# The head of a hybrid encoder kernel: x loaded by quarters of its columns and turned between the products of the first projection

## The chip, the core and the metric

The kernel runs on one core of one Trainium2 chip. The metric is the device time of one execution in microseconds (us); the time before is the median of three runs. The profile is one further execution, taken by the hardware profiler. The engines are named PE (TensorE), PEld (its weight loads), DVE (VectorE), ACT (ScalarE), POOL (GpSimd) and SP (SyncE, which here only issues transfers).

## The reference, cut to what matters

```
def _rmsnorm(x, g):
    y = xf * lax.rsqrt(jnp.mean(xf * xf, axis=-1, keepdims=True) + EPS)
    return (y * g).astype(x.dtype)

def reference(x, ...):                       # x: 1 x 512 tokens x 1024
    for layer in range(2):
        h = _rmsnorm(x, mix_norm[layer])
        if layer % 2 == 0:
            x = x + _even_mixer(h, even_w_in[j], ...)   # proj = h @ w_in (1024 x 5376), attention, out projection
        else:
            x = x + _odd_mixer(h, ...)                  # gated recurrence
        x = x + _swiglu(_rmsnorm(x, ffn_norm[layer]), ...)
    return _rmsnorm(x, final_norm)
```

In `_even_mixer` the first 768 columns of `proj` are the queries (512), key (128) and value (128) of a grouped attention whose queries and keys are RMS-normalised per head. The other 4608 columns belong to a second group of heads.

## The kernel before

All products are made in three passes: an operand is split into a rounded half (`h_hi`, `w_hi`) and the remainder (`h_lo`, `w_lo`), and `mm3` adds hi·hi, hi·lo and lo·hi into one bank of PSUM (`ps`, eight banks of 512 columns). Each engine runs its own hand-written list of instructions in order; semaphores join them.

The weights come in chunks through a ring of four: SP loads chunk c into `stage` when POOL has finished chunk c-4 (`chunk_lo`), ACT rounds it into `w_hi` (`conv`, needs the products of chunk c-4 to be over, `chunk_used`), and POOL takes the remainder `w_lo` (`lo`). Chunks 0 to 15 are the first projection: for each step k of 0 to 7, one chunk of 512 and one of 256 columns, six tiles of 128 columns and so 18 products of 128x512. Chunks 16 to 111 are four head pairs of 24 chunks each (384 columns, 9 products a chunk).

x comes as four tokens-by-1024 blocks (`x_tok`, one load per block c). PE turns each block by eight 128x128 transposes (`x_turn`), and DVE and ACT copy the turned blocks from PSUM into `x_t` (channels on partitions). The first projection works on x times the norm's gain without the norm's per-token factor: `raw_high` (ACT) and `raw_low` (DVE) make the halves of that. The factor is brought in later where the queries, keys and values are used. For the head pairs the properly normalised h is needed:

- ACT squares the four blocks of x with a running sum (`x_sq`), DVE and ACT make 1/sqrt of the mean (`rstd`), DVE spreads it on a diagonal (`spread`), and PE broadcasts it over the partitions with a product into bank 7 (L2097, after step k = 3; `first_rb`).
- DVE copies it out (`rstd_a`) and makes, for each k, `h_scaled(k)` (into a ring of three `h_f`). ACT rounds it (`high(k)`, when step k's products no longer need the raw half), and DVE takes the remainder (`h_lo_part(k)`).
- Chunk 16+k of the first pair waits for `h_lo_part(k)`.

Small parameters come by twelve loads (`params_in`) and are turned on PE after step 5 (L2100); DVE copies them (L1272, `params_ready`), and the first pair's products wait for that. Then the outputs of the first projection leave PSUM in `first_pair`: ACT copies the value (`v_f`) and the key and squares the key. DVE scales the four query tiles (`aq_f`, L1345), and ACT squares each (`sq_qk`). PE sums the squares by head with tiny products (L2111): the key's ahead of the pair's step j = 2, the first query tile's ahead of j = 3. `x_spill` stores `x_t` to memory (2 MB) behind chunk 19.

Of the kernel before, what the change touches and what calls it, by code (L numbers as in the profile page):

```python
# [226 lines left out]

SWAP_A = [(i + 16) % 32 for i in range(32)]
# [64 lines left out]
def build(nc, A, out):  # L293
# [4 lines left out]
    with ctx:  # L298
# [36 lines left out]
        x_sq = at("x_sq", Z + 16 * K, [D])  # L335
# [69 lines left out]
        consts_in, mix_in, params_in, x_in = sem("consts_in"), sem("mix_in"), sem("params_in"), [sem(f"x_in{c}") for c in range(NC)]  # L405
# [3 lines left out]
        mix_gain_in, x_by_dve, x_by_act = sem("mix_gain_in"), sem("x_by_dve"), sem("x_by_act")  # L409
# [34 lines left out]
        x_rows = A["x"][0].rearrange("(i c) d -> c i d", c=NC)  # L444
# [63 lines left out]
        def _(sync):  # L508
# [10 lines left out]
            for c in range(NC):  # L519
                sync.dma_start(x_tok[:, c, :], x_rows[c]).then_inc(x_in[c], 16)  # L520
            for c in range(C_PAIR):
                k = c // 2
                col, n = (512, 256) if c % 2 else (0, 512)
                load(c, c, stage[:, c % RING, 0:n], w_even[rows(k), col:col + n])
                if c == 4:
                    sync.dma_start(head_sel[:, :], A["consts"][:, K_HEAD:K_HEAD + 2]).then_inc(params_in, 16)
                    for at_, name, n in ((G_FFN, "ffn_norm", 16), (G_FINAL, "final_norm", 8),
                                         (CONV_W, "odd_conv_w", 32), (CONV_B, "odd_conv_b", 8), (GA_B, "odd_gate_a_b", 16),
                                         (GX_B, "odd_gate_x_b", 16), (LAM, "odd_lambda", 16)):
                        v = A[name]  # L530
# [5 lines left out]
                if c == 7:  # L536
                    sync.dma_start(tab(K_COSA, 2 * T), A["consts"][:, K_COSA:K_COSB]).then_inc(table_a_in, 16)
                if c == 9:
                    sync.dma_start(tab(K_COSB, 2 * T), A["consts"][:, K_COSB:K_MASK]).then_inc(table_b_in, 16)
                if c == 11:  # L540
                    sync.dma_start(tab(K_MASK, NC * T), A["consts"][:, K_MASK:K_ALL]).then_inc(masks_in, 16)

            for p in range(4):
                for j in range(PAIR_CHUNKS):
                    t, k = divmod(j, KD)
                    c = C_PAIR + p * PAIR_CHUNKS + j
                    dst = stage[:, c % RING, 0:384].rearrange("p (g d) -> p g d", g=3)
# [173 lines left out]
        def _(act):  # L721
# [96 lines left out]
            def raw_high(k):  # L818

                if k == 0:  # L820
                    act.wait_ge(mix_gain_in, 1)
                    act.wait_ge(x_by_dve, 3)
                act.wait_ge(x_by_act, 1 + k // 4)
                act.activation(h_hi[:, k, :], x_t[:, k, :], ACT.Copy, scale=params[:, G_MIX + k:G_MIX + k + 1]).then_inc(h_hi_done, 1)
# [8 lines left out]
            act.wait_ge(x_turned, 2)  # L833
            act.activation(x_t[:, :, P:2 * P], ps[:, 2:4, :].rearrange("p b (j t) -> p (b j) t", t=P), ACT.Copy).then_inc(x_by_act, 1)
            convs(0, 1)
            act.wait_ge(x_turned, 4)
            act.activation(x_t[:, 4:8, 3 * P:4 * P], ps[:, 7, :].rearrange("p (j t) -> p j t", t=P), ACT.Copy).then_inc(x_by_act, 1)
# [3 lines left out]
            convs(2, 4)  # L841
            for k in range(2, KD):
                raw_high(k)
            for c in range(NC):
                act.wait_ge(x_in[c], 16)
                if c:
                    act.wait_ge(first_ss, c)
                act.activation(x_sq[:, :], x_tok[:, c, :], ACT.Square, accum_out=rstd[:, c:c + 1]).then_inc(first_ss, 1)
                if c == 1:
                    convs(4, 6)  # L850
            act.wait_ge(first_ms, 1)
            act.activation(rstd[:, :], rstd[:, :], ACT.Sqrt).then_inc(first_sqrt, 1)
            for k in range(KD):
                if k:
                    convs(2 * k + 4, 2 * k + 6)
                for i in {2: (0,), 3: (1, 2), 4: (3, 4)}.get(k, (k,) if k > 4 else ()):
                    high(i)
# [354 lines left out]
        def _(dve):  # L1212
# [14 lines left out]
            def x_in_place(c):  # L1227

                dve.wait_ge(x_turned, c + 1)
                b0 = 4 if c == 2 else 6  # L1230
                V.tensor_copy(x_t[:, :, c * P:(c + 1) * P], ps[:, b0:b0 + 2, :].rearrange("p b (j t) -> p (b j) t", t=P)).then_inc(x_by_dve, 1)

            def raw_low(k):

                dve.wait_ge(h_hi_done, k + 1)
                V.scalar_tensor_tensor(out=h_lo[:, k, :], in0=x_t[:, k, :], scalar=params[:, G_MIX + k:G_MIX + k + 1],  # L1236
                                       in1=h_hi[:, k, :].bitcast(f32), op0=ALU.mult, op1=ALU.subtract).then_inc(h_lo_done, 1)
# [11 lines left out]
            x_in_place(0)  # L1249
            dve.wait_ge(mix_turned, 1)  # L1250
            V.tensor_copy(params[:, 0:G_FFN], ps[:, 1, 0:G_FFN]).then_inc(mix_gain_in, 1)
            x_in_place(2)
            dve.wait_ge(x_turned, 4)
            V.tensor_copy(x_t[:, 0:4, 3 * P:4 * P], ps[:, 6, :].rearrange("p (j t) -> p j t", t=P)).then_inc(x_by_dve, 1)
            for k in range(KD):
                raw_low(k)
            dve.wait_ge(first_ss, NC)
            V.tensor_scalar(rstd[:, :], rstd[:, :], 1.0 / D, EPS, ALU.mult, ALU.add).then_inc(first_ms, 1)
            dve.wait_ge(first_sqrt, 1)
# [10 lines left out]
            h_lo_part(KD - 2)  # L1270
            dve.wait_ge(params_turned, 1)
            step.mark(V.tensor_copy(params[:, G_FFN:P], ps[:, 6, G_FFN:P]))  # L1272
            V.tensor_copy(qk_gain[:, :], ps[:, 6, P:P + 2]).then_inc(params_ready, 1)
            h_lo_part(KD - 1)
# [770 lines left out]
        def _(pe):  # L2045
# [18 lines left out]
            def x_turn(c):  # L2064

                pe.wait_ge(x_in[c], 16)
                if c == 3:
                    pe.wait_ge(x_by_dve, 1)
                b0 = (6, 2, 4, 6)[c]
                for j in range(KD):  # L2070
                    last = pe.transpose(ps[:, b0 + j // 4, (j % 4) * P:(j % 4 + 1) * P], x_tok[:, c, j * P:(j + 1) * P], ident[:, :])
                last.then_inc(x_turned, 1)
# [4 lines left out]
            x_turn(0)  # L2077
            pe.wait_ge(mix_in, 16)
            pe.transpose(ps[:, 1, 0:G_FFN], mix_rows[0:G_FFN, :], ident[0:G_FFN, 0:G_FFN]).then_inc(mix_turned, 1)
            x_turn(1)  # L2080
            x_turn(2)
            x_turn(3)
            idle_products(6)

            for k in range(KD):
# [8 lines left out]
                if k == 3:  # L2094
                    pe.wait_ge(ones_set, 2)
                    pe.wait_ge(first_diag, 1)
                    pe.matmul(ps[:, 7, :], ones[:, :], diag[:, 0, :, :].rearrange("p c q -> p (c q)"), start=True, stop=True).then_inc(first_rb, 1)  # L2097
                if k == 5:
                    pe.wait_ge(params_in, 16 * 12)
                    pe.transpose(ps[:, 6, 0:P], p_rows[:, :], ident[:, :])  # L2100
# [447 lines left out]
```

## Time and profile before

| | |
|---|---|
| three runs | 1270.55, 1270.8, 1273.13 us; median 1270.8 |
| the profiled execution | 1271.04 us; its span 1269.2 us |
| mean granted TensorE clock | 0.996 of full speed |
| busy: PE, PEld, DVE | 1252.1 us (99%), 1003.1 (79%), 840.4 (66%) |
| busy: ACT, POOL | 663.8 us (52%), 401.9 (32%) |

Times in the rows are microseconds from the span's start, unless marked ns. A matmul's row ends later than the next one starts, since they are pipelined: the pace is the distance of the starts. What stands in brackets at the end of a row is the idle time of the engine before it, and what ended it.

### The profile page before, as it was taken

How to read it: one execution, taken by the hardware profiler on the slowest of the kernel's cores; microseconds unless marked ns; L12 is line 12 of the kernel's file. 1: busy time of each engine (PE TensorE's matmuls, PEld its weight loads, DVE VectorE, ACT ScalarE, POOL GpSimd, SP SyncE). 2: the span in 40 equal slices, each digit the busy share in tenths (PEclk: the TensorE clock that was granted, in tenths of full speed). 3: DMA queues.
4: the chain of work that ended last, by engine and by line, in shares of the span. 5: the costliest groups of instructions: out<-in, count | busy, mean ns of one | idle time of the engine just before them, and what ended most of it. 6: DMA issues, size and time to landing. Idle time of an engine off the chain costs nothing.

```text
span 1269.2 us, 17728 instructions
## 1 busy us (share of the span) xinstructions
PE 1252.1 (99%) x6473; PEld 1003.1 (79%) x6473; DVE 840.4 (66%) x1328; ACT 663.8 (52%) x1214; POOL 401.9 (32%) x327
## 2 busy tenths in 40 slices
PE   8999999999999999999999999999979999999998
PEld 6877787777778888888888887777868888888886
DVE  4965765666636889898531156999888899972211
ACT  5454444444436665655532357786556655563233
POOL 4575563645625000000344443430300000024442
PEclk9999999999999999999999999999989999999999
DMA  6522222221244432330322345224443422122232
GB/s 208 169 72 66 64 63 64 59 68 56 57 137 149 142 133 100 133 100 1 93 83 92 100 136 163 67 67 150 150 149 100 133 88 78 67 75 83 84 100 92
DMA packets 101039, 126.60 MB, mean 100 GB/s; under 512 B 5976, under 2 KB 63576, under 8 KB 100312
## 3 DMA queue, kind: packets, MB, share of 16 engines
q1 hardware_dynamic: 100920, 125.45, 30.9%
q8 instruction: 52, 0.85, 0.3%
q14 instruction: 35, 0.29, 0.1%
q10 hardware_dynamic: 32, 0.01, 0.0%
HBM read 119.15 MB, written 6.29 MB: 99 GB/s over the span
## 4 chain that ended last, share of the span: by engine, by line
PE 89%; DVE 5%; issue 2%; ACT 2%; DMA 1%; SPq 1%; POOL 0%; POOLq 0%; DVEq 0%; ACTq 0%
PE ps L2048 26%; PE ps L2050 26%; PE ps L2049 26%; PE ps L2487 2%; PE ps L2402 2%; PE ps L2146 1%; PE ps L2158 1%; PE ps L2169 1%; PE ps L2204 1%; DMA w_stage<-in_even_w_in_dram 1%; DMA w_stage<-in_even_w_out_dram 1%; PE ps L2181 1%; PE ps L2185 1%; DVE sq_sum L1310 1%; PE ps L2215 1%
## 5 line engine op out<-in xcount | busy, mean ns | idle before, releaser
L672 POOL TENSOR_TENSOR w_lo<-w_stage,w_hi 128x512 fp32r<-128x512 f32 (+2 forms) x270 | 336.0, 1250 | 851.7 <-ACT w_hi L730 851.2
L730 ACT ACTIVATE w_hi<-w_stage 128x512 fp32r<-128x512 f32 (+2 forms) x288 | 163.8, 574 | 297.8 <-PE ps L2050 279.7
L2048 PE MATMUL ps<-h_hi,w_hi 128*128 128x512 f32 x464 | 190.3, 410 | 1.5 <-DVE h_lo L1236 1.0
L2048 PE MATMUL ps<-w_hi,h_hi 128*128 128x512 f32 (+1 forms) x496 | 181.5, 366 | 6.1 <-DVE w_lo L1605 6.1
L2050 PE MATMUL ps<-h_hi,w_lo 128*128 128x512 f32 x464 | 181.2, 391 | 0.0
L2049 PE MATMUL ps<-h_lo,w_hi 128*128 128x512 f32 x464 | 181.2, 390 | 0.0
L2050 PE MATMUL ps<-w_hi,h_lo 128*128 128x512 f32 (+1 forms) x496 | 180.2, 363 | 0.0
L2049 PE MATMUL ps<-w_lo,h_hi 128*128 128x512 f32 (+1 forms) x496 | 180.1, 363 | 0.0
L2048 PE MATMUL ps<-w_hi,h_mix 128*128 128x512 f32 x320 | 124.9, 390 | 0.4 <-DVE w_lo L1605 0.4
L2050 PE MATMUL ps<-w_hi,h_mix 128*128 128x512 f32 x320 | 124.5, 389 | 0.0
L2049 PE MATMUL ps<-w_lo,h_mix 128*128 128x512 f32 x320 | 124.5, 389 | 0.0
L2048 PEld LDWEIGHTS ps<-h_hi,w_hi 128*128 128x128 f32 x464 | 87.2, 188 | 36.1 <-issue 13.8
L2048 PEld LDWEIGHTS ps<-w_hi,h_hi 128*128 128x128 f32 x496 | 93.8, 189 | 22.3 <-issue 6.5
L2049 PEld LDWEIGHTS ps<-w_lo,h_hi 128*128 128x128 f32 x496 | 94.0, 189 | 15.5
L2050 PEld LDWEIGHTS ps<-w_hi,h_lo 128*128 128x128 f32 x496 | 93.9, 189 | 14.8
L2050 PEld LDWEIGHTS ps<-h_hi,w_lo 128*128 128x128 f32 x464 | 87.1, 188 | 18.9
L2049 PEld LDWEIGHTS ps<-h_lo,w_hi 128*128 128x128 f32 x464 | 87.3, 188 | 18.0 <-issue 2.6
L740 ACT ACTIVATE w_hi<-raw_c 128x512 fp32r<-128x512 f32 x80 | 50.2, 633 | 54.8 <-PE ps L2050 24.5
L2048 PEld LDWEIGHTS ps<-w_hi,h_mix 128*128 128x128 f32 x320 | 60.1, 188 | 13.1 <-issue 0.8
L2050 PEld LDWEIGHTS ps<-w_hi,h_mix 128*128 128x128 f32 x320 | 60.0, 188 | 12.5
L2049 PEld LDWEIGHTS ps<-w_lo,h_mix 128*128 128x128 f32 x320 | 60.1, 188 | 12.3
L1605 DVE TENSOR_TENSOR w_lo<-raw_c,w_hi 128x512 fp32r<-128x512 f32 x80 | 55.2, 690 | 4.9 <-ACT w_hi L740 2.1
(299 smaller groups left out, 2320.8 us busy)
## 6 DMA issues: line engine op xcount, KB each, us to landing
w_stage<-in_ffn_w_down_dram SPq DMA_DIRECT2D x88, 256.0 KB, 2.6
w_stage<-in_even_w_in_dram SPq DMA_DIRECT2D x96, 192.0 KB, 2.5
raw_c<-in_ffn_w_gate_up_dram SPq DMA_DIRECT2D x10, 1024.0 KB, 5.3
raw_b<-in_ffn_w_gate_up_dram SPq DMA_DIRECT2D x8, 1024.0 KB, 6.2
w_stage<-in_odd_w_in_dram SPq DMA_DIRECT2D x32, 256.0 KB, 2.7
w_stage<-in_ffn_w_gate_up_dram SPq DMA_DIRECT2D x6, 1024.0 KB, 5.1
raw_d<-in_ffn_w_gate_up_dram SPq DMA_DIRECT2D x6, 1024.0 KB, 7.2
raw_f<-in_ffn_w_gate_up_dram SPq DMA_DIRECT2D x6, 1024.0 KB, 6.1
```

What stands on the lines that cost most here:

```text
L672: pool.tensor_tensor(out=w_lo[:, s, 0:n], in0=stage[:, c % RING, :][:, 0:n], in1=w_hi[:, s, 0:n].bitcast(f32), op=ALU.subtract).then_inc(c ...
L730: act.activation(w_hi[:, s, 0:n], stage[:, s, 0:n], ACT.Copy).then_inc(chunk_hi, 1)
L740: act.activation(w_hi[:, c % RING, :], unit_source(n, name, u, k), ACT.Copy).then_inc(chunk_hi, 1)
L1310: V.tensor_tensor(sq_sum[:, :], sq[:, 0, :] if j == 1 else sq_sum[:, :], sq[:, j % 2, :], ALU.add).then_inc(sq_added, 1)
L1605: V.tensor_tensor(w_lo[:, s, :], unit_source(n, name, u, k), w_hi[:, s, :].bitcast(f32), ALU.subtract).then_inc(unit_lo, 1)
L2048: pe.matmul(out_, lh, rh, start=start, stop=False, skip_group_check=skip)
L2049: pe.matmul(out_, lh, rl, start=False, stop=False, skip_group_check=skip)
L2050: return pe.matmul(out_, ll, rh, start=False, stop=stop, skip_group_check=skip)
L2146: last = pe.matmul(ps[:, hh, :], aq_f[r, p, c * P:(c + 1) * P], ak[r, p // 2, :], start=True, stop=True)
L2158: last = pe.transpose(ps[:, 2 + hh, k * P:(k + 1) * P], prob_a[:, hh, k * P:(k + 1) * P], ident[:, :])
L2402: last = pe.transpose(ps[:, fb + 2 + k % 2, c * P:(c + 1) * P], f_tokens(k, c), ident[:, :])
L2487: last = pe.matmul(ps[:, 4 + q, :], gates[:, x, 2 * m + q // 2, q % 2, :], u_f[:, 2 * m + q // 2, :], start=True, stop=True)
```

## The change

x is loaded by quarters of its columns (256 columns of all four blocks, `x_load(q)`): the first quarter ahead of the first weight chunk, the others between later chunks. The parameters and the three tables go behind later chunks. PE turns x by strips of 128 columns (`x_turn(k)`, four transposes for the 512 tokens): two strips at the start, and strip k+2 after step k, into bank 6 or 7. `raw_high` and `raw_low` read the turned strip from PSUM and no longer from `x_t`; DVE copies each strip to `x_t` behind that (`x_in_place(k)`). The squares are taken by quarters on 256 columns (16 instructions in place of 4) between the conversions, and added on DVE. The norm's broadcast on PE stands after step 5, the turning of the parameters after step 6. ACT's `high(0)` to `high(3)` stand behind chunks 16 to 18, and `high(4)` to `high(7)` behind the conversion of chunk 20.

```diff
+X_BANK = (6, 7, 6, 7, 6, 7, 6, 6)
 # SP
-            for c in range(NC):
-                sync.dma_start(x_tok[:, c, :], x_rows[c]).then_inc(x_in[c], 16)
+            def x_load(q):
+                sync.dma_start(x_tok[:, :, 256 * q:256 * (q + 1)], x_cols[q]).then_inc(x_in[q], 16)
+            x_load(0)
             for c in range(C_PAIR):
...
+                if c in (4, 6, 8):
+                    x_load(c // 2 - 1)
                 load(c, c, stage[:, c % RING, 0:n], w_even[rows(k), col:col + n])
-                if c == 4:
+                if c == 10:
...
 # ACT
-                act.activation(h_hi[:, k, :], x_t[:, k, :], ACT.Copy, scale=params[:, G_MIX + k:G_MIX + k + 1]).then_inc(h_hi_done, 1)
+                act.wait_ge(x_turned, k + 1)
+                act.activation(h_hi[:, k, :], ps[:, X_BANK[k], :], ACT.Copy, scale=params[:, G_MIX + k:G_MIX + k + 1]).then_inc(h_hi_done, 1)
...
+            first_squares(0)
             for k in range(2, KD):
                 raw_high(k)
...
+                convs(2 * k, 2 * k + 2)
+                if k in (2, 3, 4):
+                    first_squares(k - 1)
...
+            convs(C_PAIR, C_PAIR + 1)
+            high(0)
+            convs(C_PAIR + 1, C_PAIR + 2)
+            high(1)
+            high(2)
+            convs(C_PAIR + 2, C_PAIR + 3)
+            high(3)
+            convs(C_PAIR + 3, C_PAIR + 4)
...
                     conv(C_PAIR + p * PAIR_CHUNKS + j + RING)
+                    if (p, j) == (0, 0):
+                        for k in range(4, KD):
+                            high(k)
 # DVE
+            def x_in_place(k):
+                dve.wait_ge(x_turned, k + 1)
+                V.tensor_copy(x_t[:, k, :], ps[:, X_BANK[k], :]).then_inc(x_by_dve, 1)
...
+            raw_low(6)
+            x_in_place(6)
             dve.wait_ge(first_rb, 1)
             step.done(V.tensor_copy(rstd_a[:, :], ps[:, 7, :]))
             h_scaled(0)
             h_scaled(1)
-            for k in range(2, KD):
-                h_lo_part(k - 2)
+            raw_low(7)
+            x_in_place(7)
+            h_scaled(2)
+            for k in range(3, KD):
+                h_lo_part(k - 3)
                 h_scaled(k)
...
 # PE
+                for c in range(NC):
+                    last = pe.transpose(ps[:, X_BANK[k], c * P:(c + 1) * P], x_tok[:, c, k * P:(k + 1) * P], ident[:, :])
                 last.then_inc(x_turned, 1)
...
-            x_turn(2)
-            x_turn(3)
             idle_products(6)
...
-                if k == 3:
+                if k == 5:
                     pe.wait_ge(ones_set, 2)
                     pe.wait_ge(first_diag, 1)
+                    pe.wait_ge(h_lo_done, 6)
+                    pe.wait_ge(x_by_dve, 6)
                     pe.matmul(ps[:, 7, :], ones[:, :], diag[:, 0, :, :].rearrange("p c q -> p (c q)"), start=True, stop=True).then_inc(first_rb, 1)
-                if k == 5:
+                if k + 2 < KD:
+                    x_turn(k + 2)
+                if k == 6:
```

SP at the start of the program, before the change: the identity, the four blocks of x, then the first weight chunks.

```order
L518 DMA ident<-in_consts_dram 128x128
L520 DMA x_tok<-in_x_dram 128x1024 x4
L513 DMA w_stage<-in_even_w_in_dram 128x512
L513 DMA w_stage<-in_even_w_in_dram 128x256
L513 DMA w_stage<-in_even_w_in_dram 128x512
```

And with the change:

```order
L521 DMA ident<-in_consts_dram 128x128
L525 DMA x_tok<-in_x_dram 128x4x256
L516 DMA w_stage<-in_even_w_in_dram 128x512
L516 DMA w_stage<-in_even_w_in_dram 128x256
L516 DMA w_stage<-in_even_w_in_dram 128x512
L516 DMA w_stage<-in_even_w_in_dram 128x256
L525 DMA x_tok<-in_x_dram 128x4x256
```

Three of the four loads of x moved behind the first weight chunks.

DVE from the copy of the norm's broadcast (`rstd_a`) on, before the change; `h_scaled` and `h_lo_part` alternate with two of the first ahead.

```order
L1264 COPY rstd_a<-ps 128x512 [waits first_rb]
L1242 SCALAR_TENSOR_TENSOR h_f<-x_t,params,rstd_a 128x512 [waits dve_step]
L1242 SCALAR_TENSOR_TENSOR h_f<-x_t,params,rstd_a 128x512
L1247 TENSOR_TENSOR h_lo<-h_f,h_hi 128x512 [waits h_hi_done]
L1242 SCALAR_TENSOR_TENSOR h_f<-x_t,params,rstd_a 128x512
```

And with the change:

```order
L1282 COPY rstd_a<-ps 128x512 [waits first_rb]
L1256 SCALAR_TENSOR_TENSOR h_f<-x_t,params,rstd_a 128x512 [waits dve_step]
L1256 SCALAR_TENSOR_TENSOR h_f<-x_t,params,rstd_a 128x512
L1250 SCALAR_TENSOR_TENSOR h_lo<-ps,params,h_hi 128x512 [waits h_hi_done]
L1245 COPY x_t<-ps 128x512 [waits x_turned]
L1256 SCALAR_TENSOR_TENSOR h_f<-x_t,params,rstd_a 128x512
L1261 TENSOR_TENSOR h_lo<-h_f,h_hi 128x512 [waits h_hi_done]
```

The last strip's remainder and copy came in behind the broadcast; a third `h_scaled` stands ahead of the first `h_lo_part`.

ACT at the end of the first projection, before the change: the copy of the value, the key, the key's square, the conversion of chunk 20, then the squares of two query tiles.

```order
L865 ACTIVATE v_f<-ps 128x512 [waits params_ready,chunk_used]
L866 ACTIVATE k_f<-ps,qk_gain 128x512
L867 ACTIVATE sq_qk<-ps 128x512
L730 ACTIVATE w_hi<-w_stage 128x384 [waits chunk_loaded0,chunk_used]
L871 ACTIVATE sq_qk<-ps 128x512 [waits aq_scaled] x2
```

And with the change:

```order
L877 ACTIVATE v_f<-ps 128x512 [waits params_ready,chunk_used]
L878 ACTIVATE k_f<-ps,qk_gain 128x512
L879 ACTIVATE sq_qk<-ps 128x512
L738 ACTIVATE w_hi<-w_stage 128x384 [waits chunk_loaded0,chunk_used]
L846 ACTIVATE h_hi<-h_f 128x512 [waits chunk_used,h_new] x4
L883 ACTIVATE sq_qk<-ps 128x512 [waits aq_scaled] x2
```

Four roundings of the normalised h came in between the conversion of chunk 20 and the squares of the query tiles.

## Rows read from the trace of the kernel before

**Rows 1.** The page: chain of work that ended last, by engine.

```profile
PE 89%; DVE 5%; issue 2%; ACT 2%; DMA 1%; SPq 1%; POOL 0%; POOLq 0%; DVEq 0%; ACTq 0%
```

**Rows 2.** Timeline of the start: start, duration, engine, line, operation, tiles.

```profile
5.58 1.21 PE L2071 MATMUL ps<-ident,x_tok 128*128 128x128 f32 x8 [0.49 <-DMA x_tok<-in_x_dram]
...
10.16 0.63 ACT L730 ACTIVATE w_hi<-w_stage 128x512 fp32r<-128x512 f32 x1 [1.13 <-DMA w_stage<-in_even_w_in_dram]
...
10.32 1.64 PE L2062 MATMUL ps<-zeros 128*128 128x512 f32 x6
...
10.88 1.29 POOL L672 TENSOR_TENSOR w_lo<-w_stage,w_hi 128x512 fp32r<-128x512 f32 x1 [8.20 <-ACT w_hi L730]
...
12.14 0.75 DVE L1236 SCALAR_TENSOR_TENSOR h_lo<-x_t,params,h_hi 128x512 fp32r<-128x512 f32 x1 [0.85 <-ACT h_hi L824]
...
12.95 0.50 PE L2048 MATMUL ps<-h_hi,w_hi 128*128 128x512 f32 x1 [0.99 <-DVE h_lo L1236]
```

**Rows 3.** DMA issues, the first load of x: size, us to landing.

```profile
x_tok<-in_x_dram SPq DMA_DIRECT2D x1, 512.0 KB, 4.3
```

**Rows 4.** DMA issues, the tables: columns as in rows 3.

```profile
table<-in_consts_dram SPq DMA_DIRECT2D x2, 512.0 KB, 4.6
...
table<-in_consts_dram SPq DMA_DIRECT2D x1, 1024.0 KB, 7.5
```

**Rows 5.** Timeline of PE, first projection and the first pair's start.

```profile
21.86 0.47 PE L2048 MATMUL ps<-h_hi,w_hi 128*128 128x512 f32 x1 [0.41 <-POOL w_lo L672]
...
30.14 1.02 PE L2097 MATMUL ps<-diag,ones 128*128 128x512 f32 x2
...
48.31 0.50 PE L2048 MATMUL ps<-h_hi,w_hi 128*128 128x512 f32 x1
...
50.00 0.50 PE L2048 MATMUL ps<-h_hi,w_hi 128*128 128x512 f32 x1
```

**Rows 6.** Chain that ended last, 611 to 625: one turning between products.

```profile
618.57 0.44 PE ps L2402 x4
```

**Rows 7.** Busy time, 611 to 650: PE, PEld, DVE, ACT, POOL, clock, DMA.

```profile
611.00:650.00 39.00, 39.00 (x197) 32.29 (x196) 18.47 (x38) 16.28 (x29) 16.93 (x13) 1.00 0.27 82
```

**Rows 8.** Timeline of DVE from the norm's copy to the query tiles.

```profile
31.20 0.69 DVE L1264 COPY rstd_a<-ps 128x512 f32<-128x512 f32 x1 [5.71 <-PE ps L2097]
31.92 1.41 DVE L1242 SCALAR_TENSOR_TENSOR h_f<-x_t,params,rstd_a 128x512 f32<-128x512 f32 x2
...
33.98 1.80 DVE L1242 SCALAR_TENSOR_TENSOR h_f<-x_t,params,rstd_a 128x512 f32<-128x512 f32 x1
...
49.50 1.09 DVE L1247 TENSOR_TENSOR h_lo<-h_f,h_hi 128x512 fp32r<-128x512 f32 x1 [1.25 <-ACT h_hi L831]
50.51 2.71 DVE L1345 TENSOR_SCALAR aq_f<-ps,qk_gain 128x512 f32<-128x512 f32 x4
```

**Rows 9.** Busy time in the same stretch: columns as in rows 7.

```profile
31.20:51.20 20.00, 19.86 (x85) 15.32 (x84) 18.68 (x21) 10.75 (x21) 13.26 (x10) 1.00 0.56 192
```

**Rows 10.** Chain that ended last: the sums of the first query tile's squares.

```profile
56.01 0.79 PE ps L2111 x8
```

**Rows 11.** Timeline of ACT: conversion of chunk 20 and the query tiles' squares.

```profile
53.61 0.53 ACT L730 ACTIVATE w_hi<-w_stage 128x384 fp32r<-128x384 f32 x1 [2.60 <-DMA w_stage<-in_even_w_in_dram]
54.04 1.07 ACT L871 ACTIVATE sq_qk<-ps 128x512 f32<-128x512 f32 x2
```

**Rows 12.** Timeline of SP: the store of x.

```profile
45.11 0.41 SPq L552 DMA_DIRECT2D x_spill<-x_t  x1
```

**Rows 13.** Timeline of PE, second feed-forward: the longest wait of the span.

```profile
939.96 0.76 PE L2048 MATMUL ps<-w_hi,h_hi 128*128 128x512 f32 x1 [6.07 <-DVE w_lo L1605]
```

**Rows 14.** Busy time behind it: columns as in rows 7.

```profile
940.00:942.00 2.00, 2.00 (x5) 1.61 (x6) 2.00 (x3) 1.97 (x4) 0.00 (x0) 0.50 1.05 405
```

More of the change, by code:

```diff
@@ L334, in build @@
         mix_rows = at("mix_rows", Z + 110.5 * K, [P])
-        x_sq = at("x_sq", Z + 16 * K, [D])
+        x_sq = at("x_sq", Z + 16 * K, [NC, 256])
+        x_ss = at("x_ss", S + 2720, [NC, 4])
         rstd_a = at("rstd_a", Z + 20 * K, [T])
@@ L404, in build @@
         f_turned = sem("f_turned")
-        consts_in, mix_in, params_in, x_in = sem("consts_in"), sem("mix_in"), sem("params_in"), [sem(f"x_in{c}") for c in range(NC)]
+        consts_in, mix_in, params_in, x_in = sem("consts_in"), sem("mix_in"), sem("params_in"), [sem(f"x_in{q}") for q in range(4)]
         table_a_in, table_b_in, masks_in = sem("table_a_in"), sem("table_b_in"), sem("masks_in")
@@ L821, in raw_high, with first_squares @@
                     act.wait_ge(mix_gain_in, 1)
-                    act.wait_ge(x_by_dve, 3)
-                act.wait_ge(x_by_act, 1 + k // 4)
-                act.activation(h_hi[:, k, :], x_t[:, k, :], ACT.Copy, scale=params[:, G_MIX + k:G_MIX + k + 1]).then_inc(h_hi_done, 1)
+                act.wait_ge(x_turned, k + 1)
+                act.activation(h_hi[:, k, :], ps[:, X_BANK[k], :], ACT.Copy, scale=params[:, G_MIX + k:G_MIX + k + 1]).then_inc(h_hi_done, 1)
+            def first_squares(q):
+                act.wait_ge(x_in[q], 16)
+                if q:
+                    act.wait_ge(first_ss, NC * q)
+                for c in range(NC):
+                    act.activation(x_sq[:, c, :], x_tok[:, c, 256 * q:256 * (q + 1)], ACT.Square, accum_out=x_ss[:, c, q:q + 1]).then_inc(first_ss, 1)
             def high(k):
@@ L841, in _ @@
             convs(2, 4)
+            first_squares(0)
             for k in range(2, KD):
                 raw_high(k)
[L844 to L857, printed above, removed]
+                convs(2 * k, 2 * k + 2)
+                if k in (2, 3, 4):
+                    first_squares(k - 1)
+                if k == 5:
+                    act.wait_ge(first_ms, 1)
+                    act.activation(rstd[:, :], rstd[:, :], ACT.Sqrt).then_inc(first_sqrt, 1)
+            convs(C_PAIR, C_PAIR + 1)
[6 more added lines that the diff above has]
+            convs(C_PAIR + 3, C_PAIR + 4)
             def first_pair(j):
@@ L1225, in spread @@
                                        src.to_broadcast([P, n, P]), ALU.mult)
[L1227 to L1231, printed above, removed]
+            def x_in_place(k):
+                dve.wait_ge(x_turned, k + 1)
+                V.tensor_copy(x_t[:, k, :], ps[:, X_BANK[k], :]).then_inc(x_by_dve, 1)
             def raw_low(k):
                 dve.wait_ge(h_hi_done, k + 1)
-                V.scalar_tensor_tensor(out=h_lo[:, k, :], in0=x_t[:, k, :], scalar=params[:, G_MIX + k:G_MIX + k + 1],
+                V.scalar_tensor_tensor(out=h_lo[:, k, :], in0=ps[:, X_BANK[k], :], scalar=params[:, G_MIX + k:G_MIX + k + 1],
                                        in1=h_hi[:, k, :].bitcast(f32), op0=ALU.mult, op1=ALU.subtract).then_inc(h_lo_done, 1)
@@ L1247, in h_lo_part @@
                 V.tensor_tensor(h_lo[:, k, :], h_f[:, k % 3, :], h_hi[:, k, :].bitcast(f32), ALU.subtract).then_inc(h_lo_done, 1)
-            x_in_place(0)
             dve.wait_ge(mix_turned, 1)
             V.tensor_copy(params[:, 0:G_FFN], ps[:, 1, 0:G_FFN]).then_inc(mix_gain_in, 1)
[L1252 to L1255, printed above, removed]
+            for k in range(5):
                 raw_low(k)
-            dve.wait_ge(first_ss, NC)
+                x_in_place(k)
+            dve.wait_ge(first_ss, 4 * NC)
+            step.mark(V.tensor_tensor(x_ss[:, :, 0], x_ss[:, :, 0], x_ss[:, :, 1], ALU.add))
+            step.done(V.tensor_tensor(x_ss[:, :, 2], x_ss[:, :, 2], x_ss[:, :, 3], ALU.add))
+            step.done(V.tensor_tensor(rstd[:, :], x_ss[:, :, 0], x_ss[:, :, 2], ALU.add))
             V.tensor_scalar(rstd[:, :], rstd[:, :], 1.0 / D, EPS, ALU.mult, ALU.add).then_inc(first_ms, 1)
+            raw_low(5)
+            x_in_place(5)
             dve.wait_ge(first_sqrt, 1)
@@ L1266, in _ @@
             h_scaled(1)
-            for k in range(2, KD):
-                h_lo_part(k - 2)
-                h_scaled(k)
[L1270 to L1274, printed above, removed]
+            raw_low(7)
[3 more added lines that the diff above has]
+                h_lo_part(k - 3)
+                h_scaled(k)
+                if k == 4:
+                    dve.wait_ge(params_turned, 1)
+                    step.mark(V.tensor_copy(params[:, G_FFN:P], ps[:, 6, G_FFN:P]))
+                    V.tensor_copy(qk_gain[:, :], ps[:, 6, P:P + 2]).then_inc(params_ready, 1)
+            for k in range(KD - 3, KD):
+                h_lo_part(k)
             def softplus_in():
@@ L2062, in idle_products, with x_turn @@
                     pe.matmul(ps[:, 0, :], zeros[:, 0:P], zeros[:, :], start=True, stop=True)
[L2064 to L2071, printed above, removed]
+            def x_turn(k):
+                pe.wait_ge(x_in[k // 2], 16)
+                before = {2: 1, 3: 2, 4: 3, 5: 4, 6: 5, 7: 7}.get(k)
+                if before:
+                    pe.wait_ge(x_by_dve, before)
+                    pe.wait_ge(h_lo_done, before)
+                for c in range(NC):
+                    last = pe.transpose(ps[:, X_BANK[k], c * P:(c + 1) * P], x_tok[:, c, k * P:(k + 1) * P], ident[:, :])
                 last.then_inc(x_turned, 1)
```

22 lines of the change are left out of this document (10 added, 12 removed).

## The prediction

> **What bounds the kernel now.** I read the chain of work that ended last first: PE holds 89% of it [rows 1], so a microsecond counts only if PE starts earlier or waits less. Then the timeline of the start. PE turns x from 5.58, as soon as the first of four blocks is there, but the first weight chunk lies behind all 2 MB of x: ACT's first conversion begins at 10.16, when its transfer ends, POOL's remainder ends at 12.17, DVE's at 12.89, and the first product starts at 12.95 [rows 2]. From there PE runs nearly without a break to the first pair at 48.31; one wait of 0.41 us stands at 21.86 [rows 5]. The last view is DVE and ACT between 31 and 56, because the change moves work towards the place where PE takes their results.
>
> **The first product.** The first quarter of x is as large as a block was, so I let it land when the block did, at about 5.5 (4.3 us after its issue [rows 3], just ahead of the first turning [rows 2]). Chunk 0 now follows at once. Before, three blocks and chunk 0 (1792 KB) landed between 5.5 and 10.16, a pace of 385 KB/us; 256 KB take 0.7, so the chunk is there at 6.2. Conversion to the end of POOL's remainder took 12.17 - 10.16 = 2.0 us, to the end of DVE's 2.7, with a copy of x between that goes away (10.16 to 12.89 [rows 2]); this gives 8.2 to 8.9. The eight transposes of the two strips take some 1.1 (1.21 with the drain) from 5.58 and the six idle products 1.64 [rows 2], which end at 8.3. I take 8.3: **4.65 us earlier**. The other end: quarters are read in pieces of 1 KB, which no row shows. The nearest slow rows are the tables: 512 KB more took 7.5 - 4.6 = 2.9 us [rows 4], 177 KB/us, and with it the quarter and chunk 0 come 1.6 + 0.8 = 2.4 later, the first product at 10.7. I stay near the pace of x, which is the same tensor at the same moment.
>
> **The turnings in the loop.** Six of eight strips are now turned between steps. Such a piece stands in the trace already: four transposes between products cost PE 0.44 us [rows 6]. 6 x 0.44 = **2.64 us later**. They cost only that if their waits are over: strip k+2 overwrites a bank whose strip went through ACT and DVE a step (18 products, 4.1 us at 8.28 us for 36, from 21.86 to 30.14 [rows 5]) before, and on ACT the four squares of a quarter fit in the same step. The wait of 0.41 should go too, since the parameters no longer stand ahead of chunk 5 on SP: **0.4 earlier**. The pair could then start at 8.3 + (48.31 - 12.95) - 0.4 + 2.64 = 45.9, 2.4 us earlier than before.
>
> **The norm, later.** The broadcast moves from step 3 to step 5. It comes at 8.3 + (30.14 - 12.95 - 0.4) + 8.28 + five turnings (2.2) = 35.6, and DVE's copy of it, 1.06 later as before (31.20 against 30.14 [rows 5, 8]), at 36.6: 5.4 us later, though the pair starts earlier. From that copy to the end of the first scaled query tile (51.19, a quarter of 2.71 behind 50.51 [rows 8]) DVE needed 20.0 us for 18 large operations: the copy, eight `h_scaled`, eight `h_lo_part` and the tile. A large one takes 0.70 alone (1.41 for two), 12.6 in all, and 0.4 for two small copies; 1.3 was idle, waiting for ACT's last rounding. DVE was busy 18.7 [rows 9]; so 5.7 us were lost beside POOL's ten remainders in that stretch, as the row of 1.80 shows [rows 8]. In the changed order `raw_low(7)` and `x_in_place(7)` come in, 20 large ones, 14.4 us. Of POOL's remainders seven fall there, chunks 14 to 20 (chunk 21 is converted only behind the query tiles' squares), so I count 5.7 x 7/10 = 4.0. Waiting for ACT I take as half the 1.3, 0.6. The first query tile is scaled at 36.6 + 14.4 + 4.0 + 0.6 = 55.6, squared by 56.15 (0.54 each [rows 11]).
>
> PE takes that square ahead of j = 3, at 56.01 before [rows 10]: 7.7 us after the pair's start. Before, it was there at about 54.6, right behind chunk 20's conversion at 53.61, which waited for its transfer 8.5 us behind the store of x at 45.11 [rows 11, 12]. Now four roundings and DVE's chain stand between. The pair's start itself needs `params_ready`, which on DVE stands behind ten of the large operations: 36.6 + 7.4 + five of POOL's remainders (2.9) = 46.9. The value's copy then is early enough for the third tile, which waited before (50.00 [rows 5] where the pace gives 49.8). PE reaches j = 3 at 46.9 + 7.5 = 54.4 and waits 1.75 us, to 56.15. **Sum: +0.15 us at 56.01**, and nothing behind it in the pair knows that x came earlier; the store of x lies some 4 us earlier and is no longer what chunk 20 waits for. All of the gain at the front is waited off where the late norm is used.
>
> The last strip's two operations on DVE are the one price that I cannot see: they read PSUM, and beside POOL an `h_scaled` took 1.80 in place of 0.70 [rows 8]. If POOL held both as much, they would cost 2.2 more, and none of it if it held neither. The Trainium skill (SBUF — State Buffer, Who interferes with whom) says that DVE and GpSimd block each other only over a shared port pair, which a DVE operation takes with two SBUF inputs or in a two-port mode. By that, an operand in PSUM leaves these two free; the row of 1.80, with two large inputs in SBUF, agrees, and the sum would be 0.4 smaller (18/20 of the 4.0). I keep the count by rows, 4.0.
>
> **The rivals.** *The gain arrives.* If POOL takes little from DVE (say half of the 4.0, and no idle time), the query tile is squared at 53.6 and PE, which would start the pair at 45.9, needs it at 53.6: 2.4 us and the 0.2 of the third tile are won, 1268.3. For it: all short rows of DVE are 0.70. Against it: DVE had no idle time before the last rounding, and the chain starts 5.4 us later. It is at the edge of what this kernel's measurement can tell from no change (about 0.2%, 2.5 us).
>
> *Slower: the norm's chain comes out late enough to show.* Were the 20 operations to take what the 18 took on the mean, (18.7 - 0.4)/18 = 1.02 us, with the full idle time, the square would be there at 36.6 + 20.4 + 0.4 + 1.3 + 0.55 = 59.2: +3.2 us, 1274.0. It decides from 58.5 on. PE would then wait some 4.5 us, and a wait of 6.07 has let the granted clock fall to 0.50 behind it [rows 13, 14], where five products took 2 us, 0.40 each in place of 0.23; two us more are possible. For it: the masks' 1 MB, 7.5 us to landing [rows 4], now go out just ahead of chunk 16, behind which `high(0)` stands on ACT. Against it: chunk 21 and the following cannot be converted while the chain runs, so POOL rests.
>
> *The front does not come.* At the tables' pace the first product is at 10.7; all of the above moves by 2.4, and the end by about 2.5: 1273.4.
>
> *The clock.* The Trainium skill (TensorE: Matmul & The Clock Gate, PE-mode transpose) says that transposes don't keep the clock up as products do; the six turnings would then cost more than themselves. Products at 0.40 in place of 0.23 through the loop's 144 would give 24 us more, about 1295. But the turnings between products from 611 to 650 ran at a clock of 1.00 throughout [rows 7], so this has hardly a chance.
>
> **How the numbers follow.** The profiled execution took 1271.04, 0.2 above the median of the three runs, 1270.8; I add the sum to the median: 1270.8 + 0.15 = 1270.95, **1271.0**. Chances: my sum within 2.5 us 0.61; the gain arrives 0.18, half of it beyond 0.2%; the late chain 0.15, with 0.13 beyond; the slow front 0.05, half beyond; the clock 0.01. Faster 0.09 and 0.02 for what I haven't seen, 0.11; slower 0.17; same 0.72. The range reaches to the rivals on both sides, 1268.3 to 1273.7.
>
> **What would show it.** Right: the first product near 8.3; four transposes of 0.44 behind six of the steps without a wait; the norm's copy on DVE near 36.6; PE waiting 1 to 2.5 us ahead of the first query tile's sums, on ACT's square, itself behind DVE; the sums within 2 us of 56. The prediction is wrong if PE doesn't wait there (the gain then stands in full), if a turning waits for DVE or ACT in the loop, if chunk 0 or the first quarter lands after 7, or if the time moves behind the first pair.

## The result, and the profile after

The changed kernel is **slower**, by 0.46%: 1277.8 us in the median of 12 executions (1273.53 to 1280.21) against 1271.0 of before in 12 (1270.12 to 1273.13); the ratio is 1.0046, with a 95% interval of 1.0033 to 1.0059. The executions of the changed kernel differ more than those of before: four took 1273.5 to 1273.9 at a mean granted clock of 0.994, eight took 1276.5 to 1280.2 at 0.992 to 0.989. The profiled one took 1277.24, its span 1275.4: 6.2 us more than the span before.

The timeline of the changed kernel, start, duration, engine, line, operation; first PE and ACT at the start, then PE, DVE, POOL and SP up to the first query tile:

```profile
4.99 1.09 PE L2094 MATMUL ps<-ident,x_tok 128*128 128x128 f32 x8
...
5.61 0.63 ACT L738 ACTIVATE w_hi<-w_stage 128x512 fp32r<-128x512 f32 x1 [2.94 <-DMA w_stage<-in_even_w_in_dram]
...
7.77 0.47 PE L2070 MATMUL ps<-h_hi,w_hi 128*128 128x512 f32 x1 [0.29 <-POOL w_lo L680]
...
30.23 0.60 PE L2094 MATMUL ps<-ident,x_tok 128*128 128x128 f32 x4
...
34.80 1.02 PE L2120 MATMUL ps<-diag,ones 128*128 128x512 f32 x2
...
44.94 0.50 PE L2070 MATMUL ps<-h_hi,w_hi 128*128 128x512 f32 x1
...
51.94 0.40 PE L2072 MATMUL ps<-h_hi,w_lo 128*128 128x512 f32 x1
55.59 1.78 PE L2138 MATMUL ps<-head_sel,sq_qk 128*128 128x2 f32 x8 [3.26 <-ACT sq_qk L883]
...
35.86 0.69 DVE L1282 COPY rstd_a<-ps 128x512 f32<-128x512 f32 x1 [2.92 <-PE ps L2120]
36.58 1.41 DVE L1256 SCALAR_TENSOR_TENSOR h_f<-x_t,params,rstd_a 128x512 f32<-128x512 f32 x2
37.91 0.74 DVE L1250 SCALAR_TENSOR_TENSOR h_lo<-ps,params,h_hi 128x512 fp32r<-128x512 f32 x1
38.58 0.68 DVE L1245 COPY x_t<-ps 128x512 f32<-128x512 f32 x1
...
40.32 1.50 DVE L1261 TENSOR_TENSOR h_lo<-h_f,h_hi 128x512 fp32r<-128x512 f32 x1
...
50.49 1.16 DVE L1261 TENSOR_TENSOR h_lo<-h_f,h_hi 128x512 fp32r<-128x512 f32 x1 [1.62 <-ACT h_hi L846]
...
52.35 1.89 DVE L1261 TENSOR_TENSOR h_lo<-h_f,h_hi 128x512 fp32r<-128x512 f32 x3
54.16 2.72 DVE L1367 TENSOR_SCALAR aq_f<-ps,qk_gain 128x512 f32<-128x512 f32 x4
...
37.58 5.12 POOL L680 TENSOR_TENSOR w_lo<-w_stage,w_hi 128x512 fp32r<-128x512 f32 x4 [3.44 <-ACT w_hi L738]
...
40.28 0.48 SPq L560 DMA_DIRECT2D x_spill<-x_t  x1
```

The front does what it was built for. The first product starts at 7.77 in place of 12.95 [rows 2], no turning waits for anything, and the first pair starts at 44.94, 3.4 us before the 48.31 of [rows 5]. At the sums of the first query tile only 0.4 of that is left: 55.59 against 56.01 [rows 10], because PE stands still for 3.26 us in front of them. Up to there the changed kernel is no slower. Its loss stands behind that place, and the busy time by stretches shows it (columns as in rows 7; the first row is DVE's stretch from the norm's copy to the first scaled query tile):

```profile
35.86:54.84 18.98, 16.47 (x77) 12.88 (x75) 17.14 (x23) 9.97 (x19) 8.74 (x7) 1.00 0.62 203
...
52.00:54.00 2.00, 0.33 (x2) 0.00 (x0) 2.00 (x4) 0.63 (x1) 0.00 (x0) 1.00 0.35 98
54.00:56.00 2.00, 0.41 (x3) 0.41 (x3) 2.00 (x4) 1.00 (x2) 0.00 (x0) 0.93 0.00 0
56.00:58.00 2.00, 2.00 (x9) 1.90 (x10) 2.00 (x3) 2.00 (x5) 1.00 (x1) 0.50 0.00 0
...
66.00:68.00 2.00, 2.00 (x6) 1.56 (x5) 0.00 (x0) 0.00 (x0) 0.00 (x0) 0.50 0.00 0
68.00:72.00 4.00, 4.00 (x22) 3.55 (x21) 0.44 (x2) 1.67 (x5) 1.01 (x1) 0.83 0.09 24
```

The granted clock was 1.00 up to the wait, fell as PE began again, and stayed at 0.50, which is 1.2 of 2.4 GHz, for 13.6 us: 0.07/0.5 of 2 us, all of the six stretches from 56 to 68, and 0.17/0.5 of 4 us. PE was busy all through the six, but its products of 128x512 started 0.43 us apart (58.23, 58.66, 59.09), where 0.23 is the pace at full clock. Before, the clock is 1.00 in the same place:

```profile
50.00:72.00 22.00, 22.00 (x115) 18.27 (x116) 15.74 (x25) 10.83 (x25) 8.65 (x10) 1.00 0.44 124
```

While PE has work left, the only other place where the clock falls in any profile here is the wait of 6 us in the second feed-forward [rows 13]. It is in all of them, before, changed and the runs below, with the same mean of 0.83 from 930 to 950, so it makes no difference between them. What the fall at the first pair cost is read at the next place where both kernels have DVE waiting for PE: DVE takes up the finished sums at 63.67 before and at 69.89 after.

In the timeline of before:

```profile
63.67 0.20 DVE L1363 TENSOR_TENSOR rstd_qk<-ps,rstd_sq 128x40 f32<-128x40 f32 x1 [1.78 <-PE ps L2111]
```

And after:

```profile
69.89 0.20 DVE L1385 TENSOR_TENSOR rstd_qk<-ps,rstd_sq 128x40 f32<-128x40 f32 x1 [5.75 <-PE ps L2138]
```

From the first query tile's sums to there it was 63.67 - 56.01 = 7.66 us, and is 69.89 - 55.59 = 14.30: 6.6 us lost, of which the front had saved 0.4. That is the 6.2 of the span.

Why PE waited is in the chain of work that ended last (start, us, what):

```profile
30.39 0.44 PE ps L2094 x4
...
37.58 3.71 POOL w_lo L680 x3
41.31 8.03 DMA w_stage<-in_even_w_in_dram
...
49.41 0.04 ACT w_hi L738
...
49.84 0.62 ACT h_hi L846
...
50.49 1.17 DVE h_lo L1261
...
54.24 0.67 DVE aq_f L1367
...
54.94 0.61 ACT sq_qk L883
...
55.59 1.78 PE ps L2138 x8
```

The first of these rows is a turning on the path, 0.44 us. Further down, chunk 20's load was 8.03 us on its way, behind the 2 MB store of x that SP had issued at 40.28. ACT stood at that chunk's conversion until 49.41, and `high(4)` to `high(7)` are behind it in ACT's list. DVE was idle for 1.62 us until `high(4)` came (50.49), and the query tiles are behind DVE's remainders.

### The profile page after: what moved, and what is told of

Its sections match the earlier page's. It is cut to its first block, busy times and chain, and to the rows that moved or that the text cites. A ratio compares the mean times of both kernels' runs of the same rounds, so it can differ in the third digit from the quotient of the medians.

```text
span 1275.4 us, 17764 instructions
## 1 busy us (share of the span) xinstructions
PE 1256.8 (99%) x6473; PEld 1008.0 (79%) x6473; DVE 836.4 (66%) x1336; ACT 664.6 (52%) x1236; POOL 399.7 (31%) x327
## 4 chain that ended last, share of the span: by engine, by line
PE 88%; DVE 5%; issue 2%; ACT 2%; DMA 2%; POOL 0%; SPq 0%; POOLq 0%; DVEq 0%; ACTq 0%
PE ps L2070 26%; PE ps L2072 25%; PE ps L2071 25%; PE ps L2514 2%; PE ps L2429 2%; PE ps L2173 1%; PE ps L2185 1%; PE ps L2196 1%; DMA w_stage<-in_even_w_in_dram 1%; PE ps L2231 1%; DMA w_stage<-in_even_w_out_dram 1%; PE ps L2208 1%; PE ps L2212 1%; DVE sq_sum L1332 1%; PE ps L2242 1%
```

## The experiments

All ran against the kernel before, which took 1270.9 us in the median each time. The four runs that follow the changed kernel in the table were on one chip, the next three on a second and the last on a third, and the kernel before took 1270.95, 1270.92 and 1270.93 us there. Theory: the wait at the first query tile's sums eats the front's gain, and the clock that falls behind it makes the loss. Rivals: the new front (turnings, loads) lowers the clock, and the wait doesn't matter; or DVE's own work, and not the order on ACT and SP, makes the wait.

| run | median us (lowest to highest) | ratio, 95% interval | PE's wait in its profile, 44 to 72 us |
|---|---|---|---|
| changed kernel | 1277.8 (1273.5 to 1280.2) | 1.0033 to 1.0059 | 3.26 |
| PE kept busy in the wait | 1271.06 (1270.6 to 1272.3) | 0.9991 to 1.0008 | none |
| roundings first | 1270.31 (1268.3 to 1276.5) | 0.9988 to 1.0015 | 1.09 |
| store of x later | 1273.05 (1269.3 to 1279.1) | 1.0006 to 1.0039 | 1.79 |
| before, with a wait | 1277.65 (1275.1 to 1283.2) | 1.0036 to 1.0073 | 3.16 |
| the same, PE kept busy | 1274.31 (1273.8 to 1275.6) | 1.0016 to 1.0036 | none |
| roundings first, PE kept busy | 1269.47 (1268.6 to 1270.4) | 0.9978 to 0.9995 | none |
| two query tiles first | 1269.55 (1268.1 to 1272.7) | 0.9979 to 0.9997 | 0.28 and 0.51 |
| no wait | 1268.13 (1267.7 to 1269.3) | 0.9970 to 0.9989 | none |

**PE kept busy in the wait.** On PE, in the changed kernel:

```diff
+                    if j == 3:
+                        for _ in range(16):
+                            pe.matmul(ps[:, 4, 64:512], h_hi[:, 0, 0:P], h_hi[:, 0, 0:448], start=True, stop=True)
                     for t in {2: (4,), 3: (0,), 4: (1, 2), 5: (3,)}[j]:
```

Expected:

> The changed kernel with sixteen products of 128x448 (results unused) on PE ahead of its wait for the first query tile's square, so that PE is busy while it waits. Theory: in the changed kernel the wait of 3.26 us itself costs nothing against before (sums at 55.59 against 56.01), but it lets the granted clock fall to 0.50 for 13.65 us, and that costs 6.8 us. Then the sums stay at 55.5 to 56.0, the clock stays at 1.00 from 50 to 72 us, and the time is 1277.2 - 6.8 = 1270.4, the same as before. Rival (the fall of the clock comes from the turnings in the loop or from the transfers, not from the wait): the clock falls there all the same, and the time stays near 1277.8.

The timeline of PE shows the sixteen products where the wait was, and the sums no earlier:

```profile
52.43 3.41 PE L2136 MATMUL ps<-h_hi 128*128 128x448 f32 x16
55.68 0.95 PE L2141 MATMUL ps<-head_sel,sq_qk 128*128 128x2 f32 x8
```

The busy time by stretches shows the clock:

```profile
56.00:58.00 2.00, 2.00 (x13) 1.74 (x13) 2.00 (x3) 1.91 (x5) 1.02 (x2) 1.00 0.00 0
```

The sums lie where they did, the clock stays at 1.00, and the time is that of before, ratio 1.0000. The turnings, the loads and the chain behind the norm are all still there, so the rival on the front falls: the fall of the clock needs the wait, and without it the change is neutral, as 55.59 against 56.01 says.

**A wait in the kernel before.** The wait alone, without the new front; on DVE and PE:

```diff
                 step.done(V.tensor_tensor(rot_a[:, :], aq_f[:, t, :], tab(K_SINA, T), ALU.mult))
+                if t == 0:
+                    V.tensor_copy(scratch[:, 2:3], ones[:, 0:1]).then_inc(held, 1)
...
+                    if j == 3:
+                        pe.wait_ge(held, 1)
                     for t in {2: (4,), 3: (0,), 4: (1, 2), 5: (3,)}[j]:
```

Expected:

> The kernel before (x loaded by blocks and turned ahead of the loop) with one wait more: PE takes the first query tile's sums only when DVE has made the first product of that tile's rotation, which ends at 58.98 in the trace of before; a copy of one column on DVE tells PE so. Theory: PE waits some 3.3 us, from 55.85 to 59.2, the granted clock falls to 0.50 behind it, and the time grows by 3.3 for the wait and by 3.4 to 6.8 for the clock, to 1277.7 to 1281. Rival (a wait of this length alone doesn't lower the clock, the new front is needed for it): the clock stays at 1.00 and the time is near 1274.3.

The timeline of PE:

```profile
58.78 1.05 PE L2115 MATMUL ps<-head_sel,sq_qk 128*128 128x2 f32 x8 [3.16 <-DVE scratch L1331]
```

The busy time by stretches:

```profile
60.00:62.00 2.00, 2.00 (x7) 1.62 (x6) 0.66 (x1) 0.00 (x0) 0.00 (x0) 0.62 0.03 8
62.00:64.00 2.00, 2.00 (x9) 1.72 (x9) 0.00 (x0) 0.52 (x1) 0.13 (x1) 0.53 0.00 0
```

The clock fell here too, with the old front: in the profiled execution for 0.38/0.5 x 2 + 0.47/0.5 x 2 = 3.4 us, in others for longer, to go by their mean clock (the six executions run from 1275.1 at a mean of 0.996 up to 1283.2 at 0.989). The median, 6.7 us over before, is at the low edge of what the theory gave.

**The same wait, with PE busy in it.** The edits of the last two runs together:

```diff
                     if j == 3:
+                        for _ in range(16):
+                            pe.matmul(ps[:, 4, 64:512], h_hi[:, 0, 0:P], h_hi[:, 0, 0:448], start=True, stop=True)
                         pe.wait_ge(held, 1)
```

Expected:

> The run with the added wait in the kernel before, with sixteen products of 128x448 (results unused) on PE in that wait. Theory: the wait alone costs 3.2 us (PE starts the sums at about 58.9 instead of 55.85) and everything above that was the clock, which now stays at 1.00: 1271.0 + 3.2 = 1274.2 in every execution. Rival (the added wait also holds up later work, which costs the rest): 1276 to 1279 although the clock stays at 1.00.

The busy time by stretches:

```profile
60.00:62.00 2.00, 2.00 (x11) 1.68 (x11) 1.02 (x2) 0.00 (x0) 0.00 (x0) 1.00 0.05 15
62.00:64.00 2.00, 2.00 (x19) 1.94 (x17) 0.00 (x0) 0.52 (x1) 0.95 (x1) 1.00 0.00 0
```

The clock stays at 1.00 where it fell in the last run. The median is 1274.31, and the longest execution 1275.6: the wait costs 3.4 us, and the 3.3 us between this run's median and the last one's were the clock.

**Roundings first.** On ACT, in the changed kernel:

```diff
                     attention(p, j)
-                    conv(C_PAIR + p * PAIR_CHUNKS + j + RING)
                     if (p, j) == (0, 0):
                         for k in range(4, KD):
                             high(k)
+                    conv(C_PAIR + p * PAIR_CHUNKS + j + RING)
```

Expected:

> The changed kernel with ACT's four roundings high(4) to high(7) ahead of the conversion of chunk 20 in place of behind it. Theory: chunk 20's load waits 8.0 us behind the store of x, its conversion stands at the head of ACT's list until 49.41, and the roundings, DVE's remainders and the query tiles queue behind it. With the roundings first, high(4) starts near 47.1, DVE's idle 1.62 us goes, the first query tile is squared near 53.2, PE waits some 0.9 us instead of 3.26, the clock stays at 1.00, and the time is near 1268.2. Rival (DVE's own work makes the wait: two more operations, and POOL beside it): the sums of the first query tile stay later than 55, the clock falls, 1276 to 1278.

The timeline, ACT and PE:

```profile
47.15 1.19 ACT L846 ACTIVATE h_hi<-h_f 128x512 fp32r<-128x512 f32 x2
...
53.60 1.05 PE L2138 MATMUL ps<-head_sel,sq_qk 128*128 128x2 f32 x8 [1.09 <-ACT sq_qk L883]
```

`high(4)` is at 47.15, the sums at 53.60, and the wait is 1.09: the mechanism as expected, and the rival on DVE's own work explains at most what is left. The clock isn't as expected. It stayed at 1.00 in the profiled execution, 1268.76, but five of the twelve executions were within 0.6 us of 1268.3, and the others up to 8.2 us above, at mean clocks down to 0.991. The kernel before, without this wait, spreads over 3.0 us. So even a wait of 1.09 us seems to have a price in some executions; the run with PE kept busy in it, below, tests that.

**The store of x later.** On SP, in the changed kernel, so that it goes out behind chunk 21:

```diff
-                    if (p, j) == (0, 3):
+                    if (p, j) == (0, 5):
                         sync.wait_ge(x_by_dve, KD)
```

Expected:

> The changed kernel with the store of x (2 MB) issued behind chunk 21 in place of chunk 19; ACT's order is as in the changed kernel. Theory (as for the run with the roundings first): chunk 20 then lands before its slot is free, near 47, its conversion starts near 47.2 and high(4) near 47.6; the first query tile is squared near 53.7, PE waits about 1.4 us, the clock stays at 1.00, and the time is near 1268.7, unless chunk 22, now behind the store, comes later than its step at some 58.5. Rival (DVE's own work makes the wait): chunk 20 is converted early, but the sums stay later than 55, and the time stays at 1276 to 1278.

The timeline, ACT and PE:

```profile
48.38 0.53 ACT L738 ACTIVATE w_hi<-w_stage 128x384 fp32r<-128x384 f32 x1 [0.25 <-PE ps L2072]
...
55.17 1.05 PE L2138 MATMUL ps<-head_sel,sq_qk 128*128 128x2 f32 x8 [1.79 <-ACT sq_qk L883]
```

The busy time by stretches:

```profile
56.00:58.00 2.00, 2.00 (x7) 1.65 (x8) 1.96 (x4) 1.57 (x4) 1.37 (x2) 0.61 0.00 0
58.00:60.00 2.00, 2.00 (x8) 1.54 (x6) 1.93 (x4) 0.00 (x0) 0.69 (x1) 0.54 0.39 112
```

In this profile the first weight chunk came 1.1 us later and the pair started at 46.01, so places are compared from there. Chunk 20 no longer waits for a transfer, and the sums come 55.17 - 46.01 = 9.16 us behind the pair's start, against 55.59 - 44.94 = 10.65: 1.5 us less, as DVE's idle time was 1.62. So the store held chunk 20, and chunk 20 the roundings. But 1.79 us of waiting were left, behind which the clock fell to 0.50 for 0.39/0.5 x 2 + 0.46/0.5 x 2 = 3.4 us, and only one execution of twelve came out at 1269.3, the others 1.3 to 9.8 us above it. The time expected was 1268.7, and the profiled execution took 1271.54. Of the 2.8 us between, 1.1 are the later start, and 1.7 the clock (half of 3.4). The second is the same fault as with the roundings first: I had let a wait below two microseconds cost itself alone.

**Roundings first, PE kept busy.** On top of the run with the roundings first:

```diff
+                    if j == 3:
+                        for _ in range(6):
+                            pe.matmul(ps[:, 4, 64:512], h_hi[:, 0, 0:P], h_hi[:, 0, 0:448], start=True, stop=True)
```

Expected:

> The run with the roundings first, with six products of 128x448 (results unused) on PE ahead of its remaining wait of 1.09 us. That run took 1268.3 to 1268.9 in five executions and 1270 to 1276.5 in seven, with a mean clock of 0.997 in the first and down to 0.991 in the last. Theory: even this short wait lets the clock fall in some executions. Then the slow executions go, and the median is 1268.5 to 1268.9. Rival (the slow executions have another cause): the spread and the median near 1270.3 stay.

The executions now lie between 1268.55 and 1270.35. The long ones are gone (five of twelve were above 1271.7, now none of eleven), so they were the wait's, as far as two runs on different chips can show it. The median is 0.6 above what I gave. In this profile, whose execution is the median, the pair starts at 45.66 against 45.14 there, behind a first chunk that ACT could convert 0.3 us later (6.12 against 5.80); from the pair's start to the sums it is 8.5 us in both.

**Two query tiles first.** The roundings first, and on DVE the scaling of query tiles 0 and 1 ahead of the last three remainders of h:

```diff
+            query_tiles(0)
             for k in range(KD - 3, KD):
                 h_lo_part(k)
...
-                if j in (0, 1):
+                if j == 1:
+                    query_tiles(1)
```

Expected:

> The changed kernel with the roundings high(4) to high(7) ahead of the conversion of chunk 20 and, on DVE, the scaling of the first two query tiles ahead of the last three remainders of h in place of behind them. Theory: PE's wait at the first query tile's sums is all that kept the front's gain (the pair starts at 44.94 against 48.31); the first tile is then squared near 52.1, when PE comes at about 52.3, PE doesn't wait at all, the clock stays at 1.00 in every run, and the time is 1271.0 - 3.4 = 1267.6 with a spread as small as that of before. Rival (something behind the pair's start, the ring of weight chunks behind the store of x above all, holds the pair to its old time anyway): another wait of 1 to 3 us appears between 52 and 66 and the time is 1269 to 1271.

The timeline, DVE, POOL and PE:

```profile
51.47 3.52 DVE L1261 TENSOR_TENSOR h_lo<-h_f,h_hi 128x512 fp32r<-128x512 f32 x3
...
51.45 2.98 POOL L680 TENSOR_TENSOR w_lo<-w_stage,w_hi 128x384 fp32r<-128x384 f32 x2 [4.55 <-ACT w_hi L738]
...
56.33 1.05 PE L2143 MATMUL ps<-head_sel,sq_qk 128*128 128x2 f32 x8 [0.28 <-ACT sq_qk L883]
...
67.51 1.95 PE L2156 MATMUL ps<-diag,half_ones 128*128 128x512 f32 x4 [0.51 <-DVE diag L1239]
```

A miss: the wait at the first tile is gone, but other waits, as the rival had it, appeared (0.28 and 0.51 us, shorter than its 1 to 3), and the time is the rival's, 1269.55. The waits are DVE's: the three remainders took 3.52 us beside POOL, in place of 1.89 in the changed kernel, where POOL rested. The profiled execution took 1268.1 and is the shortest of the eleven, so the two waits don't explain the median; six of the others ran at mean clocks of 0.996 to 0.993 against its 0.997, and no profile shows where.

**No wait.** On top of that, three query tiles first, and DVE's softplus and the rotation of the first query tile behind the key's diagonal (which PE takes at j = 8):

```diff
-            query_tiles(0)
+            query_tiles((0, 1, 2))
...
-                if j == 3:
-                    softplus_in()
-                if j == 4:
-                    dve.wait_ge(aq_scaled, 4)
-                    aq_swap(0)
-                    aq_rope(0)
...
+                    softplus_in()
+                if j == 7:
+                    dve.wait_ge(aq_scaled, 4)
+                    aq_swap(0)
+                    aq_rope(0)
```

Expected:

> The run with two query tiles first, with three of them ahead of the last remainders of h, and with DVE's softplus and the rotation of the first query tile moved behind the key's diagonal. That run still waited 0.28 us for the third tile's square and 0.51 us for the key's diagonal, both behind DVE, and its executions took 1268.1 to 1270.05 and once 1272.7. Theory: the gain at the pair's start, 3.4 us, is only kept where PE waits nowhere behind it; then PE has no wait between 44 and 72 us, and the median is 1267.4 to 1268.2 with all executions within 1.5 us. Rival (POOL's remainders, now beside DVE's three query tiles, make other work late): a new wait between 52 and 80 us and 1268.5 to 1270.

The timeline, PE and DVE:

```profile
52.33 0.95 PE L2142 MATMUL ps<-head_sel,sq_qk 128*128 128x2 f32 x8
...
60.22 0.20 DVE L1384 TENSOR_TENSOR rstd_qk<-ps,rstd_sq 128x40 f32<-128x40 f32 x1 [0.21 <-PE ps L2142]
```

PE waits nowhere until a wait of 0.43 at 73.06, and DVE takes up the sums at 60.22, 3.45 us before the 63.67 of before. The median is 1268.13 and all executions lie within 1.7 us, as expected but for 0.1 us of spread. This version is **faster than both kernels**, than before by 0.1 to 0.3%.

## Why the prediction was wrong

The forecast was 1271.0 and the range up to 1273.7; it is 1277.8. Point by point:

- **The first product**: 7.77 instead of 8.3. Quarter and chunk 0 land at the pace of x, as chosen, and half a microsecond earlier than I let them (the turnings start at 4.99, the conversion at 5.61). The other end, the tables' pace, didn't come: over all the profiles with this front the conversion starts between 5.61 and 6.71.
- **The turnings**: 0.44 us, and no waits; right. The clock stays at 1.00 through all of them, so that rival is out.
- **The norm's chain on DVE**: the copy at 35.86 (36.6 forecast), the first query tile scaled at 54.16 + 2.72/4 = 54.84. That is 18.98 us, and the forecast had 19.0, but that is luck: its parts were wrong in opposite directions. DVE was busy 17.14 of them, so by the forecast's own count of 14.4 for the work alone POOL took 17.14 - 14.4 = 2.7 and not 4.0. DVE was idle for 1.84 and not for 0.6. The first error lies partly in the last strip's two operations, the price I couldn't see: 0.74 and 0.68 with POOL busy from 37.58 to 42.70, where the `h_scaled` and the `h_lo_part` right behind took 1.22 and 1.50. The rule of the Trainium skill that I had weighed (SBUF — State Buffer, Who interferes with whom) is borne out, and also by the three remainders above, two large SBUF inputs each, at 3.52 against 1.89.
- **"The store of x lies some 4 us earlier and is no longer what chunk 20 waits for"**: wrong. The store was indeed issued 4.8 us earlier, but chunk 20's load was still behind it, and in the new order the roundings were behind chunk 20. That made DVE's idle time. The run with the store later shows it.
- **The wait**: 3.26 us instead of 1.75, since the parameters came 2 us earlier than forecast and the pair started at 44.94 and not at 46.9, while the chain's end hardly moved. The sums came at 55.59; forecast were 56.15. In itself a longer wait in front of the same end costs nothing, as the run with PE kept busy in it shows.
- **The step that failed** is the one behind it: "PE reaches j = 3 at 46.9 + 7.5 = 54.4 and waits 1.75 us", priced as 1.75 us that the front had won anyway. I looked up the granted clock behind a wait of 6.07 us [rows 13, 14] and counted such a price only in the slower rival, with "two us more" and "from 58.5 on". The sums came 2.9 us before that point, and the clock fell all the same, for 6.6 us in the profiled execution, over three times that price. Nor would the 1.75 us that I had forecast have been free: in the run with the store later the clock fell behind 1.79 us, which cost 1.7 us in its profile, and its median is 2.1 above before.

So the slower rival had the right place (PE waiting for the late norm's chain, and the clock behind it), and the wrong point from which it decides. A wait that replaces PE's work one for one is not neutral.

What stays open is why the fall lasts longer in some executions than in others of the same kernel: 1273.5 to 1280.2 here with the same program. The clock at a place is only known for the profiled execution; for the others there is the mean.

## What to carry to other kernels

On an engine list that is nearly always busy, a gain at the front that ends in a wait further on can be worth less than nothing. Here 3.4 us won at the pair's start became 6.8 lost: the granted clock fell behind the wait, and the products there came every 0.43 us in place of 0.23. Before moving work earlier, follow the late consumer's chain through every queue in between, here a weight chunk behind a large store and four roundings behind that chunk's conversion, and move that order too. Where a wait can't be avoided, products that nobody needs, as many as fit into the wait, kept the clock at 1.00 and gave back 3.3 us in the kernel before with a wait and 6.7 in the changed one. Better still was to have no wait: only the last run kept most of the front's gain, 2.8 of 3.4 us.

## What the runs showed of the hardware that was not expected

- A wait of PE of 3.26 us, between long stretches of products at full clock, was followed by 13.6 us at a granted clock of 0.50; one of 3.16 us by 3.4 us of it in the profiled execution. With a wait of 1.79 us the profile shows 3.4 us of it too. The executions with waits of 1.79 and 1.09 us spread over 9.8 and 8.2 us, where those of before spread over 3.0; with products put into the waits of 3.26 and 1.09 us they spread over 1.7 and 1.8.
- A store of 2 MB that nothing in this stretch waited for cost through the transfer behind it: chunk 20's load took 8.03 us, where the median of these loads between 36 and 60 us was 3.0. It cost because four other instructions stood behind that load's conversion: with those ahead of it (roundings first) the first query tile's sums came 2.2 us earlier after the pair's start.
